# Two-block transformer kernel: another order of the second block's feature chunks, the first block's rotations one chunk later, and one product in place of four

## The reference, cut to what matters

```python
# block one: z = rmsnorm(h) @ w_in; q, k, v of three dilated attention groups, an RWKV-7 branch, gates
q = rope(qkv[:, :, 0], pos)          # 12 heads of 64 features
k = rope(qkv[:, :, 1], pos)          # 12 heads of 64 features
# rope: [x1 * cos - x2 * sin, x2 * cos + x1 * sin] over the halves of a head

# block two: p = rmsnorm(h) @ w_in_2, cut into q_a, k_a, v_a, q_b, k_b, v_b, q_idx, k_idx, w_idx,
# q_c, k_cmp, v_cmp, k_sel, v_sel, k_win, v_win, gates and merge gates
o_a = stick_breaking(q_a, k_a, v_a)
o_b = dsa(rope(q_b), rope1(k_b), v_b, rope(q_idx), rope1(k_idx), w_idx)
o_c = nsa(rope(q_c), rope1(k_cmp), v_cmp, rope1(k_sel), v_sel, rope1(k_win), v_win, ...)

def _compress(tok, pos_emb, w1, w2):     # of k_cmp and v_cmp: 15 blocks of 32 tokens
    blocks = tok[:, idx] + pos_emb
    hid = jax.nn.gelu(blocks.reshape(B, n_cmp, CMP_LEN * hd) @ w1)
    return hid @ w2
```

## Time and profile before

| | |
|---|---|
| timed runs (3) | 908.6 to 909.56 us, median 909.33 |
| the profiled execution | 909.91 us |
| its span, first to last instruction | 907.4 us |
| PE busy | 882.2 us, 97% of the span |
| DVE busy | 606.8 us, 67% |
| ACT busy | 480.5 us, 53% |
| POOL busy | 29.2 us, 3% |
| granted TensorE clock | 0.998 of full speed |
| moved by DMA | 150.71 MB |

### The profile page before, as it was taken

One profiled execution on the slowest core, in us unless ns is written; L12 is line 12 of the kernel. 1 busy time (PEld: TensorE's weight loads), 2 busy tenths in 40 slices (PEclk: granted clock), 3 DMA queues, 4 the chain that ended last, 5 costly groups with the idle time before them and its releaser, 6 DMA issues.

```text
span 907.4 us, 15435 instructions
## 1 busy us (share of the span) xinstructions
PE 882.2 (97%) x6552; PEld 748.8 (83%) x6552; DVE 606.8 (67%) x976; ACT 480.5 (53%) x775; POOL 29.2 (3%) x51
## 2 busy tenths in 40 slices
PE   7999999999899999999999999999999999999997
PEld 4999898787689888888889978776788788888885
DVE  4578978557856666656766577877863566666673
ACT  4775667436534444456444856484622545555561
POOL 0010000010000000000000020000000000000000
PEclk9999999999999999999999999999999999999999
DMA  9644333224468665555339764353817566665521
GB/s 336 190 140 140 99 119 114 63 83 150 178 248 282 188 190 190 200 202 187 121 112 229 164 210 144 111 186 107 277 38 206 146 187 188 191 193 194 199 95 47
DMA packets 131204, 150.71 MB, mean 166 GB/s; under 512 B 11808, under 2 KB 102176, under 8 KB 131008
## 3 DMA queue, kind: packets, MB, share of 16 engines
q1 hardware_dynamic: 129920, 145.57, 51.8%
q10 hardware_dynamic: 1216, 4.16, 1.2%
HBM read 148.67 MB, written 1.05 MB: 165 GB/s over the span
## 4 chain that ended last, share of the span: by engine, by line
PE 85%; DVE 7%; ACT 4%; issue 2%; DMA 1%; POOL 0%; POOLq 0%; ACTq 0%; DVEq 0%
PE psum L821 12%; PE psum L716 9%; PE psum L718 9%; PE psum L717 9%; PE psum L826 7%; PE psum L774 4%; PE psum L794 3%; PE psum L795 3%; PE psum L803 3%; PE psum L722 3%; PE psum L870 2%; PE psum L880 2%; PE psum L871 2%; PE psum L827 2%; DVE parts L2705 2%
## 5 line engine op out<-in xcount | busy, mean ns | idle before, releaser
L1808 ACT ACTIVATE parts<-low 128x1024 fp32r<-128x1024 f32 (+3 forms) x252 | 254.3, 1044 | 65.6 <-PE psum L718 48.3
L2705 DVE TENSOR_TENSOR parts<-low,parts 128x1024 fp32r<-128x1024 f32 (+3 forms) x156 | 183.7, 1206 | 37.7 <-ACT parts L1808 37.5
L716 PE MATMUL psum<-parts 128*128 128x512 f32 (+2 forms) x424 | 169.1, 399 | 4.6 <-DVE parts L2705 2.5
L718 PE MATMUL psum<-parts 128*128 128x512 f32 (+2 forms) x424 | 163.5, 386 | 0.0
L717 PE MATMUL psum<-parts 128*128 128x512 f32 (+2 forms) x424 | 163.4, 385 | 0.0
L1808 ACT ACTIVATE high<-psum 128x512 f32<-128x512 f32 (+6 forms) x115 | 63.4, 560 | 134.2 <-PE psum L827 76.4
L821 PE MATMUL psum<-parts 128*128 128x512 f32 x462 | 116.8, 392 | 0.0
L716 PEld LDWEIGHTS psum<-parts 128*128 128x128 f32 x424 | 79.6, 188 | 26.3 <-DVE parts L2705 4.5
L821 PEld LDWEIGHTS psum<-parts 128*128 128x128 f32 x462 | 86.9, 188 | 16.9
L718 PEld LDWEIGHTS psum<-parts 128*128 128x128 f32 x424 | 79.6, 188 | 16.4
L717 PEld LDWEIGHTS psum<-parts 128*128 128x128 f32 x424 | 79.8, 188 | 13.9
(11 more groups left out here) (313 smaller groups left out, 1310.6 us busy)
## 6 DMA issues: line engine op xcount, KB each, us to landing
low<-in_w_in_dram SPq DMA_DIRECT2D x40, 1024.0 KB, 5.3
low<-in_w_ffn_in_dram SPq DMA_DIRECT2D x44, 512.0 KB, 5.2
low<-in_w_ff_in_dram SPq DMA_DIRECT2D x16, 1024.0 KB, 5.7
low<-in_w_ff_out_dram SPq DMA_DIRECT2D x16, 1024.0 KB, 4.8
low<-in_w_ffn_out_dram SPq DMA_DIRECT2D x11, 1024.0 KB, 5.0
low<-in_w_out_dram SPq DMA_DIRECT2D x8, 1024.0 KB, 5.2
low<-in_w_ple_gate_dram SPq DMA_DIRECT2D x4, 1024.0 KB, 5.0
low<-consts_dram ACTq DMA_DIRECT2D x1, 2078.0 KB, 9.0
```

Source lines behind the costliest of these rows:

```text
L716: mm(o, l[0], r[0], start, False)
L718: return mm(o, l[1], r[0], False, stop)
L1808: return e.activation(o, a, ACT.Copy)
L2705: tt(rslot3(n, nk, width)[:, r, 0:w], slot3(n, nk, width)[:, r, 0:w], st.hi3(j)[:, r, 0:w].bitcast(F32), ALU.subtract) \
```

## The change

It has three parts.

1. **Block two's chunks.** In `plan_2` the shared chunk and the short chunk stand ahead of the last full one: q_b, q_idx, shared keys, short, q_c. The numbers in `rope_to`, `rope_read`, `rope2` and the waits follow. v's token range gets banks 5 and 6 in place of the next two of `pg`. `ahead` is gone: each split stands in its plain place, beside the chunk before. ACT's copies of keys move from behind the last feature chunk to v's read.
2. **Block one's rotations.** Rotation 0 stands behind the splits of chunk 2 and no longer of chunk 1, rotation 1 behind chunk 3, rotations 2 and 3 behind chunk 4, 4 behind chunk 5. `rt1` has four buffers.
3. **The compression's sum.** A constant of 16 columns (`C_SEL`, with a one wherever row modulo 32 is the column) lets one matmul for each of k and v do what four did. The constants grow by 128 columns of 4,284.

```diff
-        rt1 = [view3(P + 9216 + 1024 * i, 2, 256) for i in range(2)]
+        rt1 = [view3(P + 8704 + 512 * i, 2, 256) for i in range(4)]
...
         plan_2 = [([(0, 256, 0)], [128, 128]), ([(256, 256, 0)], [128, 128]), ([(768, 256, 0)], [128, 128]),
-                  ([(1152, 256, 0)], [128, 128]), ([(1476, 256, 0)], [128, 128]),
-                  ([(1024, 64, 0), (1408, 64, 64), (1860, 64, 128), (1988, 64, 192)], [128, 128]), ([(1732, 128, 0)], [128])]
+                  ([(1152, 256, 0)], [128, 128]), ([(1024, 64, 0), (1408, 64, 64), (1860, 64, 128), (1988, 64, 192)], [128, 128]),
+                  ([(1732, 128, 0)], [128]), ([(1476, 256, 0)], [128, 128])]
...
-            def token_range(st, j0, n, w, freed, late):
+            def token_range(st, j0, n, w, freed, late, banks=None):
                 nk = 8 // n
-                banks = [next(pg), next(pg)]
+                banks = banks or [next(pg), next(pg)]
...
-                yield from token_range(st2, 5, 2, 464, lambda i: [main_act.at("vt2", i), main_dve.at("vt2", i)], nothing)
+                yield from token_range(st2, 5, 2, 464, lambda i: [main_act.at("vt2", i), main_dve.at("vt2", i)], nothing, (5, 6))
...
                     q.wait_ge(*cmp_dve.at("x", h))
-                    for g in range(4):
-                        t = mm(p[:, 16 * h:16 * h + 16], hd[:, h, :], ident[:, 32 * g:32 * g + 16], g == 0, g == 3)
+                    t = mm(p[:, 16 * h:16 * h + 16], hd[:, h, :], const(C_SEL, 16), True, True)
...
-            def ahead(st, j):
-
-                return st.tag == "st2" and j == 5
-
             def feature_chunk(st, j, widths, read):
                 steps = 1 + len(widths)
                 for n in range(steps):
-                    if n == 1 or n == 0 and not ahead(st, j + 1):
+                    if n < 2:
                         split(st, j + 1, (n,))
                     yield
                 q.wait_ge(*main_pe.at(st.tag, j, 1))
-                if ahead(st, j + 2):
-                    split(st, j + 2, (0,))
                 read()
                 yield
...
             def rope_read(tag, n, m, b, zs, dst):
-                if n >= (2 if tag == "qk" else 4):
-                    q.wait_ge(*rope_dve.at(tag, n - 2))
+                if n >= 4:
+                    q.wait_ge(*rope_dve.at(tag, n - (4 if tag == "qk" else 2)))
...
             def read_vt(i, p):
+                if i == 0:
+                    q.wait_ge(*rope_dve.at("in2", 4))
+                    for m, half in enumerate(half_rows[::-1]):
+                        copy(RC[half, 7, :], RC[half_rows[1], 6, :]).then_inc(key_act.up(m), 1)
+                    q.wait_ge(*key_act.at(1))
+                    copy(RC[half_rows[1], 6, :], RC[half_rows[0], 6, :]).then_inc(key_act.up(2), 1)
                 copy(vt[:, i, 0:256], p[:, 0:256])
...
+            turned_at = ((), (), (0,), (1,), (2, 3), (4,))
...
-                    yield from feature_chunk(st1, QK_AT + n, [128, 128], (lambda n=n: rope1(n - 1)) if n else nothing, nothing)
+                    yield from feature_chunk(st1, QK_AT + n, [128, 128], lambda n=n: [rope1(m) for m in turned_at[n]], nothing)
```

More of the change, by code:

```diff
@@ L83, in shape_constants @@
     c[0:64, C_SINC:C_SINC + 256] = np.concatenate([-sin, sin])
+    c[:, C_SEL:C_SEL + 16] = r % 32 == s[:, 0:16]
     return c
@@ L1884, in feature_chunk, with token_range @@
                 q.wait_ge(*main_pe.at(st.tag, j, 1))
-                if ahead(st, j + 2):
-                    split(st, j + 2, (0,))
                 read()
                 yield
-            def token_range(st, j0, n, read):
+            def token_range(st, j0, n, read, banks=None):
                 nk = 8 // n
-                banks = [next(pg), next(pg)]
+                banks = banks or [next(pg), next(pg)]
                 for s in range(n):
@@ L1895, in token_range @@
                         for r in range(nk // 2):
-                            if i == 0 and (r == 1 or r == 0 and not ahead(st, j0 + s + 1)):
+                            if i == 0 and r < 2:
                                 split(st, j0 + s + 1, (r,))
@@ L2376, in main_b @@
                     yield from feature_chunk(st2, n - 2, plan_2[n][1], lambda: read2(n, b))
[L2377 to L2383 removed]
+                yield from token_range(st2, 5, 2, read_vt, (5, 6))
             turns.alone(main_b())
@@ L2742, in feature_chunk, with token_range @@
                 yield
-            def token_range(st, j0, n, read, late):
+            def token_range(st, j0, n, read, late, banks=None):
                 nk = 8 // n
-                banks = [next(pg), next(pg)]
+                banks = banks or [next(pg), next(pg)]
                 for s in range(n):
```

32 lines of the change are left out of this document (13 added, 19 removed).

## The result

The changed kernel takes 912.49 us (median of 6 runs, 911.75 to 914.46) against 909.52 for the kernel before in the same session: ratio 1.0037, 95% interval 1.0026 to 1.0048. It is slower by 3 us. I had forecast 907.9 and a range up to 909.6.

What follows compares the result with a forecast made beforehand. PE, busy 97% of the span, was taken as the bound. Terms -1.36 - 0.4 + 0.4 + 0 = -1.4 us took the profiled 909.91 to 908.5; that execution lay 0.58 over the median, so 907.9, range 906.0 to 909.6.

Steps and rivals of the forecast that it cites:

- Block one, -1.36: Block one: with the rotation out of DVE's way ahead of its masks, PE starts its second group 1.36 us earlier.
- their cover: Block one's fourth level: DVE idles 2.62 us waiting for PE, so a further 1.93 us rotation fits with 0.7 left.
- everything is ready: Block one, first L1203: PE would arrive at 104.83 instead of 105.87 and have to wait for nothing.
- The wait of 2.7 us: Block two, ahead of the last full chunk: new PE wait of 2.7 us for DVE's split of its first half.
- 516.2: Block two: time at which PE starts the last full chunk, in place of 513.5.
- The wait in v: Block two, v's token range: PE waits 0.7 us for v's second chunk where 1.49 was.
- The shared chunk's load, +0.4: Block two: load moved from fourth to third place lands late, costing 0.4 us, bounds 0 and 0.95.
- Block two's -0.4: Block two's projection: three PE waits turn into two, first gate starts at 533.1 against 533.53, gain 0.4 us.
- The selection product, 0: Compression's product: PE arrives 1.3 us sooner but waits as much longer for ACT and DVE; worth 0, bounds -1.3 and 0.
- with the earlier shifts: Compression: the 579.60 start, where PE's L1632 waits for DVE, moves by no more than the earlier shifts.
- third rival: Block two: the shared chunk's pieces load in earnest only at 498.1, PE loses 3.1 us; 910.7 us, chance 0.08.

Runs made afterwards that it cites:

- p2: Kernel before with only block one's later rotations (four buffers, new order of rotations): 909.04 us, ratio 0.9997 to the kernel before.
- x3: Changed kernel with both halves of the last full chunk's split ahead of ACT's read of the shared chunk, its products in bank 7: 909.09 us, ratio 0.9994.
- p12: Changed kernel with the old summing product of 8 multiplications, so block two's and block one's parts alone: 914.87 us, ratio 1.0057.
- y5: p2 with 64 tiny multiplications at PE's start: 909.74 us, ratio 1.0004 to the kernel before.
- p1: Kernel before with block two's part alone (new chunk order, v in banks 5 and 6, no half split ahead): 913.26 us, ratio 1.0041.
- p3: Kernel before with the selection product alone (2 for 8 multiplications, constants 128 columns wider): 909.42 us, ratio 0.9998.
- x4: Kernel before, in its old order, with v's two tiles in banks 5 and 6 alone: 911.53 us, ratio 1.0023.
- y6: Kernel before with 64 tiny multiplications at PE's start and nothing else: 909.64 us, ratio 1.0002.
- z3: Kernel before with 32 tiny multiplications at PE's start alone: 908.41 us, ratio 0.9985.
- z2: p2 with 32 tiny multiplications at PE's start: 906.57 us, ratio 0.9967 to the kernel before.
- z1: x3 with 32 tiny multiplications at PE's start: 904.25 us, ratio 0.9938 to the kernel before.
- z4: Changed kernel with 32 tiny multiplications at PE's start: 908.15 us, ratio 0.9985 to the kernel before.
- z5: z1 with the compression's weights loaded behind the shared chunk's instead of ahead: 903.76 us, ratio 0.9938 to the kernel before.
- y2: Changed kernel with the shared chunk's weights in one load of 256 neighbouring columns instead of four of 64: 911.01 us, ratio 1.0017 to the kernel before.
- x1: Changed kernel with 20 unused multiplications of 256 columns filling PE's wait ahead of the last full chunk: 910.80 us, ratio 1.0011 to the kernel before.
- x2: Changed kernel with 20 unused multiplications of 16 columns in PE's wait ahead of the last full chunk: 910.45 us, ratio 1.0014 to the kernel before.
- z6: Changed kernel with 16 tiny multiplications at PE's start: 908.96 us, ratio 0.9996 to the kernel before.
- y7: x3 with 64 tiny multiplications at PE's start: 910.10 us, ratio 1.0004 to the kernel before.

## Why the prediction was wrong

**Block one, -1.36: right in what it removes, wrong in what it leaves.** DVE's masks, the two rotations at the fourth level and their cover (0.40 left, 0.7 forecast) are as I had them. The step that failed is "everything is ready". PE's two waits had covered the time in which it would have stood for instructions, and they came to the front: 0.84 was left in the changed kernel, 0.30 in p2 (498.85 for 499.15), and even that is not firm. The kernels with the later rotations and unmoved stands have this landmark anywhere from 498.31 (the changed kernel) over 498.95 (x3) to 499.87 (p12) and 500.26 (y5); those without them (before, p1, p3, x4, y6) at 498.91 to 499.15. With the instruction loads moved, the part is worth 497.60 - 496.29 = 1.31 (z3 against z2), and 1.84 by the medians; z1, z4 and z5, at 496.82, 496.77 and 496.47, show 0.8 to 1.1. I asked whether the 1.36 survives and looked for engines and loads of data alone; the earlier trace rows come from a timeline that had two "issue" stands further on, and I passed over them.

**The wait of 2.7 us: right**, in its cause too, DVE's split of the first half. It is 2.67. My 516.2 for its end left out block one and the load; with what these came to, -0.84 and +0.96, it would be 516.3, and it is 516.42. The wait in v is 0.55 for 0.7.

**The clock: missed.** Once its work had begun, PE was nowhere idle as long as this wait in the kernel before (1.75 us at most), and I carried the durations of the earlier trace rows over unchanged. It cost 1.3 to 1.4 in the profiled execution; what it costs in the median is not shown.

**The shared chunk's load, +0.4: the range was right (0 to 0.95), the value was not.** It measured 0.96 in y2 against the changed kernel, at the upper bound. The Trainium skill's "DMA: Bandwidth & Descriptors", by which I had estimated 0.8 from its sections "Specifications" and "Why small descriptors are slow (HBM only)", was nearer than my choice; but one load of 1 KB rows in its place removes the number of loads together with the row size, so the run does not tell those two apart.

**Block two's -0.4.** With the load and the clock taken out of the +2.15 of the stretch, -0.2 is left (2.15 - 0.96 - 1.35).

**The selection product, 0: right**, in p3: its query-key products of 579.35 start 34.95 us behind the weight product, as before. PE's waits grew by 0.8 us, where I had said 1.2.

**What no term had: the stand in the weight product, +1.91.** The forecast of 579.60 moving "with the earlier shifts" failed by just this. In the kernel before, the instruction load starts 3.0 us ahead of the weight product (541.6), and ahead of the 1 MB weight load. In the changed kernel it starts 1.1 us behind the product's start (547.0), at the weight load's end; x4 did the same with no more than the banks. The weight load itself keeps its place, its first packet comes 2.3 us ahead of the product in all three. What tips the instruction load to one side or the other is not shown. From the weight product's start to the query-key products all kernels without the stand take 34.9 to 35.0 us (before, p2, p3, x1, x2, y5, y6 and z1 to z6), those with it 36.6 to 36.9 (the changed kernel, p1, p12, x3, x4, y2, y7).

The sum is -0.84 + 0.96 + 1.35 - 0.16 + 1.91 = +3.2 between the two profiled executions, where I had -1.4. Had the instruction loads been out of the way in both kernels, the change would have come to nothing: z4 908.15 and z3 908.41 in the same session. By the medians of that session block one's part is worth -1.8 there (z2 against z3), and the rest of the change costs +1.6 (z4 against z2), in the profiled execution by the load and the clock. My third rival named the slower side by the load alone, at 910.7 and 0.08; the stand for instructions was in none of them.

## What to carry to other kernels

Removing a wait ahead of a run of short products is worth its length only if the instructions are there. Look for "issue" stands near it, and for 1 MB loads of data at the time of the instruction loads. Where a kernel's time moves by 1 to 2 us with edits that should be neutral, shift its instruction loads by half of one with a few small multiplications at the start that nobody reads, and compare both versions with and without; a comparison at one phase alone mixes the edit with its luck. And a wait that is moved into one piece can cost more than its length, by the granted clock of what follows.

## What the runs showed of the hardware

- TensorE's instructions come in loads of 16 KB, 256 instructions (52 for 13,104 multiplications and weight loads, 53 with 256 more). All 42 stands of TensorE of 0.24 to 1.57 us that no engine ended, in runs of short products of fourteen kernels, ended 2.2 to 2.6 us after the start of such a load that came with the last packets of a 1 MB weight load; not every load that came so was followed by one (z3's at 544.69 was not). 32 small multiplications at the start, 128 instructions, took the kernel before from 1 to 0.9985 and the changed one from 1.0037 to 0.9985.
- An fp32 multiplication leaves two in the profile, each with a weight load (64 of them: 6680 for 6552 multiplications, and as many weight loads).
- TensorE's granted clock was 0.50 after it had stood 2.66 or 2.67 us (changed kernel, p1, p12, y2, z4, and twice in z6), and also where 20 multiplications of 16 columns ran in most of that time (x2); with 20 of 256 columns it stayed at 1.00 (x1). It was 1.00 after TensorE had stood 2.14 (x4). The length of the last stand does not settle it alone: after 1.80 us at 230.4 in y2 it was 0.50, after 1.83 at the same place in z1 1.00:

```profile
231.00:233.00 2.00, 2.00 (x6) 1.56 (x5) 1.97 (x4) 1.74 (x3) 0.00 (x0) 0.50 1.03 396
```

- Four loads of 256 KB with rows of 256 B landed between 0.3 and 2.9 us too late for ScalarE in kernels that issue them at the same place, and in time where they were issued earlier (z5). One load of 1 MB at that place was in time in the kernel before and in y2, and 0.57 late in x4.
